# Routing steps of a mixture-of-experts layer redone: router on the residual, column groups, first expert's rows by a product

## The reference, cut to what matters

```
h = rms_norm(x, norm_ffn)
g_logits = h @ router_group_w + router_group_b          # 4 groups
g_idx = argmax(g_logits);  g_w = softmax(g_logits)[g_idx]
e_logits = (h @ router_expert_w + router_expert_b)[g_idx]   # 4 experts inside the group
top_w, top_i = top_k(softmax(e_logits), 2);  top_w /= sum(top_w)
expert_id = g_idx * 4 + top_i
y = sum over the two experts of g_w * top_w * down(silu(gate(h)) * up(h))
x = x + y
```

## Time and profile before

| | |
|---|---|
| median of 3 runs | 910.5 us (909.81 to 911.17) |
| the profiled execution, its own time | 910.69 us |
| its span in the profile | 908.9 us |
| PE busy | 789.1 us, 87% |
| DVE busy | 368.6 us, 41% |
| ACT busy | 229.9 us, 25% |
| POOL busy | 65.1 us, 7% |
| chain that ended last | PE 60%, DVE 8%, ACT 6%, issue 3%, DMA 2%, POOL 1% |
| projections | 0 to about 275 us |
| attention with output products | about 275 to 522 us |
| last output product and routing of tiles 2 and 3 | 522 to 579 us |
| experts | 579 to about 875 us |
| last gather, final norm, store | about 875 to 909 us |

### The profile page before, as it was taken

One profiled execution on the slowest core, in us unless ns is written; L12 is line 12 of the kernel. 1 busy time (PEld: TensorE's weight loads), 2 busy tenths in 40 slices (PEclk: granted clock), 3 DMA queues, 4 the chain that ended last, 5 costly groups with the idle time before them and its releaser, 6 DMA issues.

```text
span 908.9 us, 10934 instructions
## 1 busy us (share of the span) xinstructions
PE 789.1 (87%) x4021; PEld 417.8 (46%) x4021; DVE 368.6 (41%) x829; ACT 229.9 (25%) x574; POOL 65.1 (7%) x89
## 2 busy tenths in 40 slices
PE   5988999999986988899789993699999999999940
PEld 2455464456443335455455552345454545454410
DVE  4421023651205756666565634362232223222307
ACT  1211111112213455655655511001010101011104
POOL 0111001200000000000100102100000000000024
PEclk9999999999995999988998995699999999999985
DMA  8257713272359300000000026459999999999845
GB/s 293 70 158 210 249 66 120 70 231 94 129 150 307 134 1 2 1 24 1 1 24 1 6 111 208 151 211 369 388 369 400 382 397 382 399 388 395 301 144 207
DMA packets 84999, 171.46 MB, mean 189 GB/s; under 512 B 8730, under 2 KB 23802, under 8 KB 84914
## 3 DMA queue, kind: packets, MB, share of 16 engines
q1 hardware_dynamic: 76130, 153.81, 48.2%
q0 software_dynamic: 3488, 11.09, 3.5%
q10 hardware_dynamic: 5328, 5.86, 1.9%
HBM read 151.70 MB, written 21.13 MB: 190 GB/s over the span
## 4 chain that ended last, share of the span: by engine, by line
PE 60%; DVE 8%; ACT 6%; issue 3%; DMA 2%; POOL 1%; SPq 0%; ACTq 0%; DVEq 0%; POOLq 0%
PE bank L2140 20%; PE bank L2131 8%; PE bank L2530 6%; PE bank L1644 5%; PE bank L2512 4%; PE bank L1579 4%; ACT reg L1077 2%; PE bank L1598 2%; PE bank L2159 2%; DVE st L1255 2%; PE bank L1658 1%; PE bank L2123 1%; ACT work L2384 1%; PE bank L1625 1%; PE bank L1581 1%
## 5 line engine op out<-in xcount | busy, mean ns | idle before, releaser
L2140 PE MATMUL bank<-reg,qsbT 128*64 128x256 f32 (+1 forms) x704 | 187.1, 481 | 1.7 <-ACT qsbT L1882 0.8
L2530 PE MATMUL bank<-reg 128*128 128x512 f32 (+1 forms) x384 | 168.1, 584 | 2.5 <-DVE work L1211 1.3
L2140 PEld LDWEIGHTS bank<-reg,qsbT 128*64 128x64 f32 (+1 forms) x704 | 87.1, 162 | 93.2 <-issue 80.0
L2530 PEld LDWEIGHTS bank<-reg 128*128 128x128 f32 x384 | 72.7, 198 | 72.7 <-issue 69.2
L2512 PE MATMUL bank<-cf,reg 128*128 128x128 f32 (+1 forms) x424 | 68.9, 293 | 22.5 <-DVE reg L2459 9.5
L1644 PE MATMUL bank<-reg 128*128 128x512 f32 (+1 forms) x160 | 81.8, 624 | 0.0
L2512 PEld LDWEIGHTS bank<-cf,reg 128*128 128x128 f32 (+1 forms) x424 | 49.7, 150 | 46.5 <-issue 33.3
L2131 PE MATMUL bank<-reg,work 128*128 128x512 f32 x160 | 70.8, 595 | 0.0
L2384 ACT ACTIVATE work<-bank 128x128 f32<-128x128 f32 (+6 forms) x123 | 46.7, 418 | 53.2 <-PE bank L2512 31.3
L2006 DVE TENSOR_SCALAR work<-work 128x512 f32<-128x512 f32 (+1 forms) x16 | 6.0, 377 | 106.3 <-ACT work L1888 106.3
L2131 PEld LDWEIGHTS bank<-reg,work 128*128 128x128 f32 x160 | 29.6, 190 | 34.1 <-issue 33.9
(11 more groups left out here) (301 smaller groups left out, 887.4 us busy)
## 6 DMA issues: line engine op xcount, KB each, us to landing
reg<-w_gate SPq DMA_DIRECT2D x16, 2048.0 KB, 12.6
reg<-w_up SPq DMA_DIRECT2D x16, 2048.0 KB, 17.5
reg<-w_down SPq DMA_DIRECT2D x16, 2048.0 KB, 17.7
reg<-w_in SPq DMA_DIRECT2D x4, 2048.0 KB, 9.7
expert_rows<-ksbT SPq DMA_DIRECT2D x10, 512.0 KB, 15.6
expert_rows<-vsb SPq DMA_DIRECT2D x8, 512.0 KB, 5.1
reg<-cache_sb_k SPq DMA_DIRECT2D x16, 256.0 KB, 2.9
reg<-cache_sb_v SPq DMA_DIRECT2D x16, 256.0 KB, 3.4
```

The lines of the kernel that those rows point to most:

```text
L2140: ins = T.matmul(bank[which][rows, 0:w], rowsT[b][:, k, 0:n], weights[b][which][:, k, h * w:(h + 1) * w], start=(k == 0), stop=(k == KD - 1))
L2530: ins = nc.tensor.matmul(at("m", ("proj", n))[:, 0:w], hT[:, k, i * P:(i + 1) * P], win[:, pos % 2, k, 0:w], start=(k == 0), stop=(k == KD ...
```

## The change

What it does:

- PE transposes the residual `x` itself, not `h2`. The gain `norm_ffn` is multiplied into the router weights once (`wr`, one DVE step at `scale_wout`, `gainR` loaded by one more DMA with 4-byte elements), and the inverse root is applied to the logits (`scalar_tensor_tensor` with `small[..12:13]`).
- Order of a tile's routing: `transpose_ffn` (gap 0), `ffn_rows` (gap 0, behind it), `route_parts` (gap 2), `route_choice` (gap 3), `rank` (gap 5), `route_weights` (gap 7). At tiles 2 and 3 after the attention the transposes come first too.
- The router product has the weights (padded from 20 to 32 columns) as stationary operand and 128 tokens as moving columns, in four column groups of the array, two accumulating products in each (`parts`). ACT copies that result, and one product with a constant `fold` adds the groups and turns it back (`logit`).
- The choice is one DVE block of 12 instructions up to `onehot`; softmax weights are made later (`slots` and `weights`). ACT waits for DVE once in a tile, in `slots`, in place of twice.
- `base16` is added by a PE product in place of a DVE step.
- Rows of expert 0: DVE makes `rows0` for every tile, PE multiplies it by the token numbers (`ids0`, 10 one-column products), and POOL gathers expert 0's rows before the last tile's scatters. The other 15 gathers still wait for `idx`.
- Expert 1's gate and up are loaded after expert 0's rows have landed, in front of its down.

```diff
     def place_route(i, first):
-        for f, gap in zip((ffn_rows, transpose_ffn, route_group, route_experts, route_choice, rank), (0, 2, 3, 4, 5, 7)):
+        for f, gap in zip((transpose_ffn, ffn_rows, route_parts, route_choice, rank, route_weights), (0, 0, 2, 3, 5, 7)):
...
     step("expert0_down")
+    transpose_ffn(QT - 2)
     ffn_rows(QT - 2)
     mix_stats(QT - 1)
     for n in range(16):
...
         if n == 5:
-            transpose_ffn(QT - 2)
+            route_parts(QT - 2)
         if n == 8:
-            route_group(QT - 2)
-            route_experts(QT - 2)
             route_choice(QT - 2)
+        if n == 12:
+            rank(QT - 2)
         if n == 15:
-            rank(QT - 2)
-    step("expert1_gate")
+            route_weights(QT - 2)
+    transpose_ffn(QT - 1)
     ffn_rows(QT - 1)
-    transpose_ffn(QT - 1)
-    route_group(QT - 1)
-    route_experts(QT - 1)
+    route_parts(QT - 1)
     route_choice(QT - 1)
     rank(QT - 1)
+    route_weights(QT - 1)
...
     def rank(i):
         use("t", ("rank", i), "dve")
         step("rank", i)
+        sg.mark("rows0", i)
+        if i == QT - 1:
+            use("x", ("ids0",), "dve")
+            step("ids0")
+            sg.mark("ids0", 0)
+        step("slots", i)
...
     def load_router(sp):
+        sp.wait_ge(sg["zero"], 1)
+        sp.dma_start(gainR[:, :], a["norm_ffn"][0].rearrange("(k p) -> p k", p=P), allow_slow_non_contiguous=True
+                     ).then_inc(sg["router_in"], 16)
...
+        elif kind == "parts":      # ACT
+            sg.wait(act, "t_full", ("parts", i))
+            nc.scalar.copy(parts[:, 0:r], at("t", ("parts", i))[:, 0:r]).then_inc(sg["t_act"], 1)
+        elif kind == "slots":      # ACT
+            sg.wait(act, "r_max", i)
+            nc.scalar.activation(rt[0:r, 84:88], rt[0:r, 32:36], ACT.Exp, bias=rt[0:r, 72:73],
+                                 accum_out=rt[0:r, 73:74])
+            nc.scalar.activation(rt[0:r, 75:76], rt[0:r, 74:75], ACT.Exp).then_inc(sg["r_exp"], 1)
...
+        elif kind == "choice":     # DVE
+            V.scalar_tensor_tensor(rt[0:r, 16:36], at("t", ("logit", i))[0:r, 0:20], small[0:r, 12:13], br[0:r, :],
+                                   ALU.mult, ALU.add).then_inc(sg["t_dve"], 1)
+            link(V.max(m8, gl))
+            link(V.max_index(smi[0:r, 0:8], m8, gl))
+            link(V.tensor_copy(rt[0:r, 80:81], smi[0:r, 0:1]))
+            link(V.tensor_scalar(other, c["group16"][0:r], rt[0:r, 80:81], NEG, ALU.not_equal, ALU.mult))
+            link(V.tensor_tensor(el, other, ex, ALU.add))
+            link(V.max(n8, el))
+            link(V.max_index(smi[0:r, 8:16], n8, el))
+            link(V.tensor_copy(expert[0:r, i, :], smi[0:r, 8:10]))
+            link(V.tensor_tensor(chosen[0:r, i], ...is_equal))
+            V.tensor_tensor(onehot[0:r, i, :], chosen[0:r, i, 0], chosen[0:r, i, 1], ALU.add
+                            ).then_inc(sg["onehot"], 1)
...
+        elif kind == "ids0":       # DVE
+            sg.wait(dve, "x_full", ("ids0",))
+            V.tensor_copy(first_ids[:, :], bank[7][:, 0:1]).then_inc(sg["x_dve"], 1)
+            sg.wait(dve, "x_dve", ("ids0",))
+            V.memset(smi[:, 41:42], 0).then_inc(sg["ids0"], 1)
...
+        elif kind == "parts":      # PE
+            for half in range(2):
+                for q in range(4):
+                    ins = T.matmul(at("t", ("parts", i))[32 * q:32 * q + 32, 0:r], wr[:, 4 * half + q, :],
+                                   h2T[:, 4 * half + q, 0:r], start=(half == 0), stop=(half == 1))
+            ins.then_inc(sg["t_full"], 1)
+        elif kind == "choice":     # PE
+            sg.wait(pe, "t_act", ("parts", i))
+            T.matmul(at("t", ("logit", i))[0:r, 0:20], parts[:, 0:r], c["fold"], start=True, stop=True
+                     ).then_inc(sg["t_full"], 1)
...
-        elif kind == "expert1_gate":
-            sg.wait(sp, "m_full", ("wout", QT - 1, 3))
-            load_gate_up(sp, 1, 1, sg["e_wgu1"])
         elif kind == "experts":
             sp.wait_ge(sg["e_x0"], 16)
+            load_gate_up(sp, 1, 1, sg["e_wgu1"])
             load_down(sp, 1, 1, sg["e_wd1"])
...
+        if kind == "ids0":         # POOL
+            sg.wait(pool, "ids0", 0)
+            pool.wait_ge(sg["st_h2"], sg.total["st_h2"])
...
+            nc.gpsimd.indirect_dma_start(rows_in[0], None, h2_dram,
+                                         bass.IndirectOffsetOnAxis(ap=first_ids[:, 0:1], axis=0)
+                                         ).then_inc(sg["e_x0"], 16)
```

More of the change, by code:

```diff
@@ L94, in host_constants @@
         "turn": np.tile([turn(j) for j in range(NE)], (P, 1)),
+        "group16": np.tile(np.arange(16) // 4, (P, 1)),
+        "fold": (p[:, None] % 32 == np.arange(20)[None]),
         "base16": np.tile(np.arange(16) * CAP, (P, 1)),
@@ L526, in body @@
     rt = sb("rt", [P, 256])
+    parts = sb("parts", [P, P])
+    rows0 = sb("rows0", [P, TILES, P], BF16)
     weight = sb("weight", [P, TILES, 2])
@@ L582, in transpose_ffn, with route_parts, route_choice @@
             tstep("h2T", i, half)
-    def route_group(i):
-        use("t", ("logit", i), "dve")
[L586 to L596, removed]
+    def route_parts(i):
+        use("t", ("parts", i), "act")
+        step("parts", i)
+        sg.mark("parts", i)
+    def route_choice(i):
+        use("t", ("logit", i), "dve")
+        step("choice", i)
         sg.mark("onehot", i)
@@ L814, in more_transposes @@
             b4 = b[:, 0:4 * r].rearrange("p (k t) -> p k t", k=4)
-            moves = [(b4[:, k, :], h2[0:r, (4 * half + k) * P:(4 * half + k + 1) * P]) for k in range(4)]
+            moves = [(b4[:, k, :], x[0:r, i, (4 * half + k) * P:(4 * half + k + 1) * P]) for k in range(4)]
             return moves, [(h2T[:, 4 * half:4 * half + 4, 0:r], b4, 1.0)]
@@ L989, in gps_more @@
     def gps_more(pool, kind, key):
-        if kind == "rank":
+        if kind == "slots":
             i, = key
@@ L1647, in pe_more @@
                 ins.then_inc(sg[ring + "_full"], 1)
-        elif kind == "route":
+        elif kind == "parts":
+            i, = key
+            r = ROWS[i]
+            acquire(pe, "t", ("parts", i))
+            for half in range(2):
+                wait_transposed(pe, ("h2T", i, half))
+            for half in range(2):
+                for q in range(4):
[3 more added lines that the diff above has]
+        elif kind == "choice":
             i, = key
@@ L1651, in pe_more @@
             acquire(pe, "t", ("logit", i))
-            b = at("t", ("logit", i))
-            if i == QT:
-                pe.wait_ge(sg["router_in"], 64)
-            for half in range(2):
-                wait_transposed(pe, ("h2T", i, half))
-            for k in range(KD):
-                ins = T.matmul(b[0:r, 0:20], h2T[:, k, 0:r], wr[:, k, :], start=(k == 0), stop=(k == KD - 1))
-            ins.then_inc(sg["t_full"], 1)
+            sg.wait(pe, "t_act", ("parts", i))
+            T.matmul(at("t", ("logit", i))[0:r, 0:20], parts[:, 0:r], c["fold"], start=True, stop=True
+                     ).then_inc(sg["t_full"], 1)
+        elif kind == "ids0":
+            acquire(pe, "x", ("ids0",))
+            token2 = c["token2"].rearrange("p (i n) -> p i n", i=TILES)
+            for n, i in enumerate(tile_order):
+                sg.wait(pe, "rows0", i)
+                for part in range(2):
+                    ins = T.matmul(bank[7][:, 0:1], rows0[0:ROWS[i], i, :], token2[0:ROWS[i], i, part:part + 1],
+                                   start=(n == 0 and part == 0), stop=(n == TILES - 1 and part == 1))
+            ins.then_inc(sg["x_full"], 1)
         elif kind == "rank":
@@ L1664, in pe_more @@
             b = at("t", ("rank", i))
+            T.matmul(b[0:r, 0:16], ident[:, 0:r], c["base16"], start=True, stop=False)
+            done = tile_order[:tile_order.index(i)]
+            for j in done:
+                T.matmul(b[0:r, 0:16], c["onesb"][0:ROWS[j], 0:r], onehot[0:ROWS[j], j, :], start=False, stop=False)
             sg.wait(pe, "onehot", i)
[L1666 to L1670 removed]
+            T.matmul(b[0:r, 0:16], c["earlier"][0:r, 0:r], onehot[0:r, i, :], start=False, stop=True
                      ).then_inc(sg["t_full"], 1)
@@ L1838, in expert_gps @@
             pool.wait_ge(sg["ids"], 1)
-            pool.wait_ge(sg["st_h2"], sg.total["st_h2"])
-            sg.wait(pool, "pv", turned[-1])
-            sg.wait(pool, "t_full", ("logit", QT - 1))
-            for j in range(NE):
+            for j in range(1, NE):
                 if j >= 2:
```

121 lines of the change are left out of this document (51 added, 70 removed).

## The result

The changed kernel takes 915.17 us (median of 11 runs, 911.5 to 923.01), the kernel before 909.81 beside it (11 runs): a ratio of 1.0071, 95% interval 1.0043 to 1.0098. A second set gave 1.0066 (1.0044 to 1.0089). I forecast 905.9 with 899.5 to 911.5: wrong, and on the wrong side.

What follows compares the result with a forecast made beforehand. It took PE and DMA to bound the experts, a chain of small steps the routing tail, and engines waiting for each other the attention. Tail −4.4 and attention −0.2 us gave −4.6: forecast 905.9 us, range 899.5 to 911.5.

Steps and rivals of the forecast that it cites:

- the prediction's own signs: Tail forecast wrong if gate starts over 31 or under 26 us behind tile 3's last `x` add; attention, if add over 3 from 546.
- Part 6: Attention, tiles QT, 0 and 1: late-root losses against router and clock gains, sum −0.2 us, bounds −4 to +6.
- rival 3: Attention: the clock falls all the same, tiles 0 and 1 keep slow stretches, 5.3 us back: 911.2; chance 0.09.
- rival 2: Attention: the late root costs full price, 3.8 us more than counted: 909.7; chance 0.13.
- Part 1: Tiles 2 and 3 after the attention: earlier transposes and new router bring tile 3's logits at 551.9 instead of 557.74.
- Part 3: Tail: expert 0's rows gathered early by a product, at 561.1 in place of 576.36, nearly all of that hidden.
- Part 4: Tail: second scatter 559.0 in place of 564.26, table read 2.85 us later at 561.9, landed 567.1 with 2.0 for load.
- Rival 4: Tail: table read stuck behind expert 1's weights, gate 5.7 us later than before: 916.0; chance 0.08.
- Part 5: Tail: DVE's `extra` runs until 574.1 and delays its row copy; gate starts at 574.9, 4.4 us sooner than before.
- Sum: Whole kernel: −4.4 in the tail and −0.2 in the attention make −4.6 us, forecast 905.9, chance 0.50.

Runs made afterwards that it cites:

- the repaired kernel: Changed kernel with the inverse root first, the overflow arithmetic late and, where the old router was tried, slots and scatters ahead of expert 0's gather: 905.93 and 903.25 us.
- e3_early_load: Changed kernel with expert 1's gate and up loaded early again, behind tile 3's last output product: 919.33 us.
- h2_router_alone: Changed kernel with only the router undone: 16 matmul entries of 20 columns, no column groups, `parts` copy or fold: 915.93 us, 1.0074.
- f3_table_first: Changed kernel with root first and overflow arithmetic late, plus tile 3's slots and scatters ahead of expert 0's product and gather: 905.93 us, 0.9930; repeated 903.25, 0.9929.
- f4_no_ids0: Changed kernel with root first and overflow arithmetic late, but without expert 0's product; its rows gathered after the table: 907.01 us.
- g2_read_first: Table-first kernel (root first, overflow arithmetic late) with expert 0's gather behind the issue of the table read: 902.97 us.
- h1_all: Changed kernel with root first, overflow arithmetic late, table first, gather behind the read, exponentials one slot later and old router: 902.25 us, 0.9902.
- the repeated change: The changed kernel run once more, unaltered, against the kernel before: 916.13 us, 1.0066.

## Why the prediction was wrong, point by point

By the prediction's own signs both halves failed: gate starts 31.1 and 31.6 us behind the last `x` add (its bound was 31), and that add is 12.6 and 6.3 us from 546 (its bound was 3).

- **Part 6, the failed step.** It set a late root (4.9 us for three tiles) against what the router in column groups gives back (6.3), and came to −0.2. The loss was right in mechanism and about right in size: 4.0 and 2.7 us by the medians, 5.0 by stretch B. The gain of 6.3 was not there: undoing the groups changes neither the change (1.0074, where this step asked for 921 to 922 us and 915.9 came) nor the repaired kernel. I priced PE's time from the router to the `vsb` product as if PE set the end, though my own first paragraph says that no engine there is full; only 1.2 us of the 4.9 were set against DVE's longer block. What I expected of the clock behind the router (a fall with 20 columns, none with groups) held in nearly every trace and did not matter. So rival 3 did not come where it was placed, and rival 2 had the root's full price, but kept the gain beside it.
- The idle gaps: the Trainium skill ("TensorE: Matmul & The Clock Gate", section "HAM oscillation — how this bites in real kernels") lays the falls to gaps between bursts. In after PE idles 2.82 us at tile 1's `vsb` product and the following products run at 1.00; at 458.7 to 461.3 it idles 2.58, and the clock is at 0.50 when it goes on. The one fall in tile 1's router of before (0.51 in 488 to 489) has PE busy. The traces fit neither the page's reading nor mine alone.
- **Part 1:** the `x` add itself did not come sooner, since B lost more; from `x` add to second scatter I had 13.15, measured 12.8 and 12.6.
- **Part 3** was right where it said that the early gather is hidden; it left out that the gather, put ahead on POOL, delays the table beyond its own issue: its landing releases the weights' load just before the scatters are complete.
- **Part 4** took 2.85 us from scatter to read out of a trace where no gather stood ahead and no load started before the scatters were complete; it is 5.2 and 6.1 in the changed kernel. It had both times beside each other, 561.2 for the load and 561.9 for the read, and charged the load to the read alone. That is 2.4 to 3.3 us on the path, and the second failed term. The loaded read at 5.1 was right: 5.39 and 5.13, of 3.08 unloaded. Rival 4 did not come.
- **Part 5** was right: PE idles 4.10 us for DVE, and moving the block gave 3.0 in C. I wrote the remedy down as a cost and no more.
- **Sum.** Of 4.6 us, C gave 0.9 to 1.4 in place of 3.5; B in place of −1.1 lost 5.0 to the root and some 1.5 more: +5.4 by the medians. The 1.5 (216.1 in B with the root first against 214.6 in a single trace of before) is open; DVE's longer block is a candidate, argued and not shown; ACT's wait for `slots` (10 to 11 us against 7.9) is a weak one, since taking it away did not shorten B. Of the 10.0 us between forecast and result the missing gain of the router is 6.3, the tail 2.1 to 2.6. The chance of 0.09 for slower was far too small: a gain on an engine that is not full should not have outweighed the loss of a late root.

## What to carry to other kernels

When work is moved ahead of a small step on a shared engine, ask who waits for that small step: two copies in front of a 0.2 us root cost this kernel 3 to 5 us. Time saved on an engine that idles anyway, clock included, was worth nothing here; count it only where a trace shows that this engine ends the stretch. And issue first the short transfers that others wait for, and ask what the landing of a long one releases: the same gather cost 2 us ahead of the scatters and gained 2 to 3 behind them.

## What the runs showed of the hardware

Two scatters of 128 indices have their last packet 1.7 to 2.0 us behind the second issue (2.5 in e3_early_load, beside a late gather), each packet 4 or 32 bytes and 0.01 us. They complete 0.5 to 1.3 us later, but 3.2 to 4.2 later in the six traces where the first packets of a weight load were already under way.

Those first packets, one of 2 KB on each of the 16 engines, took 2.7 to 3.6 us in these six (2.4 to 2.6 in h2_router_alone, where they start as the scatters complete; 1.9 to 2.4 in e3_early_load, where the load at 547.17 comes right behind tile 2's scatters). The first 16 of the same load took 0.1 to 0.4 in before, f3_table_first, f4_no_ids0, g2_read_first and h1_all, where they do not start behind scatters. So a high DMA share need not mean much data. Stretches of the repeated change (columns: stretch, length, busy by engine, PEclk, DMA share, GB/s):

```profile
567.00:569.00 2.00, 0.00 (x0) 0.00 (x0) 0.00 (x0) 0.00 (x0) 0.00 (x0) 0.50 1.57 16
569.00:571.00 2.00, 0.00 (x0) 0.00 (x0) 0.00 (x0) 0.00 (x0) 0.01 (x1) 0.50 0.04 8
571.00:573.00 2.00, 0.00 (x0) 0.00 (x0) 0.00 (x0) 0.00 (x0) 0.56 (x1) 0.50 0.95 358
```

A packet's whole time counts where it starts, so the share is above 1 in the first row and near 0 in the second, while the same packets still run. Whether the unfinished scatters hold these packets or the packets hold the scatters' completion is open.

A table read of 8 KB took 2.5 to 3.1 us with no other transfer ahead of it, 4.2 to 4.8 behind a gather on its queue, and 5.1 to 6.6 beside 2 to 6 MB of weights.
